# Router rows of twelve tiles: a store, four quarter loads and a VectorE transpose in place of eight TensorE transposes

## The reference, cut to what matters

```python
h2 = rmsnorm(x, g_ffn).reshape(b * s, d)          # (2048, 1024)
logits = h2 @ w_router                            # (2048, 64), float32
scores = sigmoid(logits); idx = top_k(scores + router_bias, 8)
# rows of h2 are then gathered by expert; shared expert and routed experts read h2
```

## Time and profile before

| | us |
|---|---|
| median of three runs | 2726.22 (2724.84 to 2729.26) |
| the profiled execution, its own time | 2727.88 |
| span of the profiled execution | 2726.2 |

### The profile page before, as it was taken

The page is one execution under the profiler, slowest core; times in us unless marked ns, Lnnn a source line. Parts: engine busy times, 40 slices in busy tenths (PEclk is TensorE's granted clock), DMA queues, the critical chain, the costliest instruction groups (busy, mean ns, idle before and its releaser), DMA issues.

```text
span 2726.2 us, 51142 instructions
## 1 busy us (share of the span) xinstructions
PE 2622.2 (96%) x11902; PEld 2165.7 (79%) x11903; DVE 1795.3 (66%) x2519; ACT 1222.6 (45%) x1738; POOL 1311.7 (48%) x1111
## 2 busy tenths in 40 slices
PE   7999999999999999938999999999999999999997
PEld 6888888878887888736888888888888888888885
DVE  4544555646555655557777887777877777777576
ACT  3223323222323223215666665665666655556422
POOL 3000003200122013167877887787887877878711
PEclk9999999999999999959999999999999999999998
DMA  8223433442343333427898998888988988888665
GB/s 314 94 94 107 146 101 100 124 146 92 100 131 116 124 109 108 147 77 256 266 276 240 295 269 242 239 247 255 278 265 240 274 235 239 235 235 243 185 244 195
DMA packets 169902, 523.52 MB, mean 192 GB/s; under 512 B 37706, under 2 KB 43516, under 8 KB 169856
## 3 DMA queue, kind: packets, MB, share of 16 engines
q1 hardware_dynamic: 95776, 344.42, 35.3%
q0 software_dynamic: 65872, 164.37, 25.3%
q10 hardware_dynamic: 8208, 14.16, 1.5%
HBM read 434.94 MB, written 119.18 MB: 203 GB/s over the span
## 4 chain that ended last, share of the span: by engine, by line
PE 48%; DVE 2%; issue 2%; POOL 1%; DMA 1%; ACTq 1%; ACT 1%; DVEq 0%; POOLq 0%; another core or an unknown queue 0%; SPq 0%
PE ps_gu L1479 10%; PE ps_gu L1481 10%; PE ps_gu L1480 10%; PE ps_y L1481 5%; PE ps_y L1480 5%; PE ps_y L1479 5%; PE ps_h L1526 1%; POOL xs L1414 1%; ACTq L1638 1%; DVE xt L1671 0%; DVE xl L1682 0%; DMA xs<-h_dram,gidx 0%; ACT xh L1556 0%; DVE y L1743 0%; DVE expert_raw L1743 0%
## 5 line engine op out<-in xcount | busy, mean ns | idle before, releaser
L1414 POOL DMA_INDIRECT xs<-h_dram,gidx x656 | 819.8, 1250 | 202.1 <-issue 199.0
L1479 PE MATMUL ps_gu<-expert_hi,xl 128*128 (+1 forms) x1392 | 544.1, 391 | 22.6 <-DVE xl L1682 18.1
L1481 PE MATMUL ps_gu<-expert_hi,xh 128*128 (+1 forms) x1392 | 544.1, 391 | 0.0
L1480 PE MATMUL ps_gu<-expert_lo,xh 128*128 (+1 forms) x1392 | 543.5, 390 | 0.0
L1666 DVE TENSOR_TENSOR expert_lo<-expert_raw,expert_hi 128x1024 f32 (+1 forms) x390 | 459.5, 1220 | 120.3 <-ACT expert_hi L1556 82.7
L923 DVE TENSOR_TENSOR ul<-raw,uh 128x1024 fp32r<-128x1024 f32 x186 | 227.9, 1225 | 403.5 <-ACT uh L747 381.0
L1556 ACT ACTIVATE expert_hi<-expert_raw 128x1024 f32 (+1 forms) x390 | 390.6, 1051 | 62.7 <-PEq L1530 38.5
L94 POOL TENSOR_SCALAR rstd<-mean 128x1 f32<-128x1 f32 x45 | 11.1, 246 | 826.6 <-ACT junk L766 812.6
L510 PE MATMUL ps_t<-hh,ul 128*128 128x512 f32 x1024 | 402.7, 393 | 3.1 <-DVE wgl L1152 3.1
L511 PE MATMUL ps_t<-hl,uh 128*128 128x512 f32 x1024 | 400.3, 391 | 0.0
L512 PE MATMUL ps_t<-hh,uh 128*128 128x512 f32 x1024 | 400.0, 391 | 0.0
(11 more groups left out here) (266 smaller groups left out, 3940.0 us busy)
## 6 DMA issues: line engine op xcount, KB each, us to landing
expert_raw<-experts SPq DMA_DIRECT2D x396, 512.0 KB
raw<-units SPq DMA_DIRECT2D x192, 512.0 KB
xs<-h_dram,gidx POOLq DMA_INDIRECT x656
h_dram<-h ACTq DMA_DIRECT2D x17, 512.0 KB
acc_odd<-h POOLq DMA_DIRECT2D x17, 512.0 KB, 14.6
acc<-x SPq DMA_DIRECT2D x4, 2048.0 KB, 8.2
expert_raw<-acc_odd SPq DMA_DIRECT2D x16, 512.0 KB, 4.7
expert_raw<-x POOLq DMA_DIRECT2D x14, 512.0 KB, 3.7
```

The lines of the kernel that those rows point to most:

```text
L1414: nc.gpsimd.indirect_dma_start(xs[s][:, g * DQ:(g + 1) * DQ], None, h2_quarters, bass.IndirectOffsetOnAxis(ap=gidx[s][:, g:g + 1], axis=0) ...
L1479: nc.tensor.matmul(out_, sl, vh, start=first, stop=False)
L1480: nc.tensor.matmul(out_, sh, vl, start=False, stop=False)
L1481: return nc.tensor.matmul(out_, sh, vh, start=False, stop=last)
```

## The change

The twelve tiles in the loops no longer use TensorE to be turned. When `h2` is written, GpSimd stores it to its place in DRAM, waits for that store, and loads it back into `h2` by four DMAs, one for each quarter of the columns, so that row quarters and column quarters lie as a 32x32 block transpose wants them. VectorE then writes `h2t` by one transpose (`y_turn`), after the third `split_lo` of half d = 0. The router weights for these tiles lie in the matching order; SyncE loads the plain order again before the last four tiles, which are turned as before.

```diff
 (SyncE, after the last chunk's unit loads)
+            sp.wait_ge(logits_done, NT - TT + 1)
+            carry(sp, marks)
+            sp.dma_start(wr[:, :, :], w_router[1]).then_inc(wr_in, 16)
 (GpSimd)
+            def y_rows(n):
+                pool.wait_ge(y_normed, n + 1)
+                carry(pool, marks)
+                pool.dma_start(h2_tiles[ds1(n)].rearrange("a p d -> p (a d)"), h2[:, :]).then_inc(h2_stored, 16)
+                pool.wait_ge(h2_stored, n * 16 + 16)
+                carry(pool, marks)
+                for q in range(Q):
+                    pool.dma_start(h2[q * P // Q:(q + 1) * P // Q, :].rearrange("p (g d) -> p g d", g=Q),
+                                   h2_tiles[ds1(n), :, q * D // Q:(q + 1) * D // Q].rearrange(
+                                       "a (g p) d -> p (a g) d", g=Q)).then_inc(h2_quartered, 16)
             def routed(before):
                 n = before * TT
                 y_norm(n)
+                y_rows(n)
                 with pool.Fori(0, TT - 1) as i:
                     y_norm(i + (n + 1))
+                    y_rows(i + (n + 1))
                     scatter(i + n)
 (TensorE, front)
-                        if before is not None and d == 0:
-                            turn_y(i + before * TT)
 (TensorE, tail)
+                pe.wait_ge(wr_in, 16)
                 turn_y(n)
 (ScalarE, front; y_copy stays for the last four tiles)
-                        if before is not None and d == 0:
-                            y_copy(i + before * TT)
 (VectorE)
             def y_scale(i, n, col=YCOL):
                 dve.wait_ge(y_rstd, n + 1)
-                dve.wait_ge(h2_out, n * 16 + 16)
+                dve.wait_ge(h2_out, 16 * max(n - (NCH - 1) * TT, 0) + 16 if isinstance(n, int) else 16)
+            def y_turn(n):
+                dve.wait_ge(h2_quartered, n * 64 + 64)
+                dve.wait_ge(logits_done, n + 1)
+                V.transpose(h2t[:, :, :].rearrange("p k (g t) -> p g k t", g=Q),
+                            h2[:, :].rearrange("p (g k t) -> p g k t", g=Q, k=KD)).then_inc(y_copied, 1)
                         split_lo(ub + (k + 4), k + 2)
+                        if before is not None and d == 0:
+                            y_turn(i + before * TT)
 (host layout)
-        "w_router": np.ascontiguousarray(slices(a["w_router"])),
+        "w_router": np.stack([quarters(a["w_router"]), slices(a["w_router"])]),
```

More of the change, by code:

```diff
@@ L283, in route @@
         y_copied = sem("y_copied")
+        h2_stored = sem("h2_stored")
+        wr_in = sem("wr_in")
+        h2_quartered = sem("h2_quartered")
         logits_done = sem("logits_done")
@@ L351, in _ @@
                              (iota_e, iotas[1, :, 0:NE]),
-                             (gffn, g_ffn), (wr, w_router), (rbias, router_bias)):
+                             (gffn, g_ffn), (wr, w_router[0]), (rbias, router_bias)):
                 sp.dma_start(dst[tuple(slice(None) for _ in src.shape)], src).then_inc(const_in, 16)
@@ L781, in y_copy @@
             def y_copy(n):
-                act.wait_ge(y_turned, n + 1)
+                act.wait_ge(y_turned, n - (NCH - 1) * TT + 1)
                 act.wait_ge(logits_done, n + 1)
@@ L787, in y_copy @@
                 last.then_inc(y_copied, 1)
-                act.dma_start(h2_tiles[n] if isinstance(n, int) else
-                              h2_tiles[ds1(n)].rearrange("a p d -> p (a d)"),
-                              h2[:, :]).then_inc(h2_out, 16)
+                act.dma_start(h2_tiles[n], h2[:, :]).then_inc(h2_out, 16)
             def score(n):
@@ L912, in _ @@
             score(n + 3)
-            act.wait_ge(h2_out, 16 * NT + 16)
+            act.wait_ge(h2_out, 16 * TT + 16)
         @block.vector
```

## The result

The changed kernel takes 2838.87 us (median, 2837.32 to 2843.26) against 2726.54 before: ratio 1.0416, 95% interval 1.0403 to 1.0428. It is 112 us slower; the forecast was +67, with a range up to 2822. The direction and the place were right, the size was not. Its profiled execution has a span of 2841.4 us, 115.2 more than that of the kernel before.

The account below looks back on a forecast made before the run. TensorE, busy 96% of the span, was taken to bound the kernel. Nine tiles at 5.95 us (53.6) and three at 4.35 (13.0) add 66.6 to 2727.9: 2794.5 profiled, forecast 2793 us, range 2761 to 2822.

Parts of the forecast that it names:

- transposes removed: On TensorE in the loops: eight transposes a tile gone, 0.88 us saved in each of 12 tiles, 10.6 us.
- place behind the split, first tiles: At the router: the transpose queued on VectorE behind the third `split_lo` makes it 3.73 us late in three tiles.
- split and round trip, second and third tiles: At the router: 3.73 us late behind the split, plus 1.2 us for the trip through DRAM.
- the same, fourth tiles: At the router: again 3.73 us behind the split plus 1.2 us for the DRAM trip, no longer than in other tiles.
- clock: TensorE behind each stall: granted clock falls to 0.50, losing 1.5 us in three tiles and 1.9 in nine.
- Traffic and scatters: 12 MB of added DMA and the previous tile's scatters, now later on GpSimd, were to cost nothing.
- The trip in an undisturbed tile: Store of `h2` to DRAM and four quarter loads back, until VectorE wakes: 10.2 us, bounds 7.7 and about 13.5.
- VectorE's wake: Last step of the DRAM trip, VectorE starting after the quarter loads land: an estimate of 0.3 us.
- the 0.6 us that the prediction allowed for this: GpSimd's store issue under `split_lo`: if VectorE locks out descriptor writing, up to 0.6 us more in nine trips.
- nine wait 10.2 - 9.0 = 1.2 us more: At the router: the DRAM trip, 10.2 us against 9.0 available, adds 1.2 us (0 to 4.5) in nine tiles.
- Rival (D): The DRAM trip is long, 13 us, as quarters land late or issues stretch: +96, 2822 us; chance 0.17.
- 0.09 more for the change of shape: On TensorE after the transposes: the second matmul follows after 0.32 us, usually 0.23; counted in the 0.88 us removed.

Follow-up runs that it names:

- experiment 4: The changed kernel with VectorE's transpose one place earlier, ahead of the third split of half d = 0: 2824.46 us, ratio 1.0365 against the kernel before.
- (5): The kernel before, with the store moved to GpSimd and four quarter loads into a buffer that nothing reads, TensorE's transposes kept: 2728.66 us, ratio 1.0010.
- experiment 1: The changed kernel with SyncE's 2 MB residual load issued behind the first two unit loads of `back`: 2819.22 us, ratio 1.0332 against the kernel before.
- Experiment 3: The changed kernel with TensorE waiting at the same place, but running the next gate unit before the router: 2830.58 us, ratio 1.0376 against the kernel before.

## Why the prediction was wrong

Its steps, with what the trace and the runs put in their place:

| step | forecast, us | measured, us |
|---|---|---|
| transposes removed | -10.6 | -9.6 (six branch units wait for a split, 0.16 each) |
| place behind the split, first tiles | 3 x 3.73 | 3 x 3.80 |
| split and round trip, second and third tiles | 6 x 4.93 | 32.7 (31.7 idle and 6 x 0.16) |
| the same, fourth tiles | 3 x 4.93 | 39.6 (39.1 idle and 3 x 0.16) |
| clock | 21.6 | 39.6 |
| sum | +66.6 | +113.7, of 115.2 between the two spans |

**What held.** The router stands still in all twelve tiles. The wait has two causes and they divide as stated: experiment 4 takes it out of first tiles alone, of two of the three. Traffic and scatters cost nothing that can be told (5). The trip in an undisturbed tile was sized within 0.6 us, and not by errors that cancel: 0.81 us to the store, 4.67 from there to the first quarter load and 5.36 to the transpose, against 0.6, 4.4 and 5.2. The 0.3 us for VectorE's wake among these had no row. The store took 0.62 to 0.68 us to issue, also beside the split, against 0.63 in the earlier trace rows: the 0.6 us that the prediction allowed for this did not come.

**The first step that failed: the round trip of the fourth tiles.** The prediction set "nine wait 10.2 - 9.0 = 1.2 us more". Six do, about (1.3 to 1.7); three wait 8.9 to 9.6. I had bounded the trip by landings read elsewhere and had looked at the DMA share of the first iteration only the earlier trace rows. What SyncE issues meanwhile, a unit load and behind it the 2 MB residual load, I had not followed, although the residual load waits for the same count as the changed kernel's own round trip. The trace of the kernel before shows it in the fourth iteration, 6.0 us after `h2` is written at 504.48:

```profile
510.47 0.01 SPq L371 DMA_DIRECT2D x<-x  x1
```

By the steps of the prediction the quarter loads would have been issued from 504.48 + 0.6 + 3.8 + 0.6 = 509.5 to 511.1, on both sides of it. Rival (D) had the right kind of cause, a long trip, but spread evenly and not at a named place: 24.8 us were missing here, and experiment 1 gives them back (23 us).

**The second: the size of the clock's fall.** Mechanism and sign were right; "1.5 us for each of the three and 1.9 for each of the nine" came from two stalls in `back`. Here the low clock holds for about 6.5 us in the first tile, and 3.3 us are lost in the mean of the twelve, 18 us more than forecast in sum. In `back` the eight transposes of 128 columns and then full units followed; here 16 matmuls of 64 columns did. Experiment 3 puts a full unit first, and the loss falls to 1.8 in the first tile, as in `back`, 2.6 in the second and 29.6 in all, so this is 10 of the 18 us. Where the other 8 come from, and why single tiles lose from 1.7 to 4.2 with the same order of work, stays open.

**A small one: the removed transposes.** The 0.88 us took "0.09 more for the change of shape" as gone with them. In six of the twelve tiles the branch unit starts 0.16 us late all the same, because it now waits for VectorE's split: 9.6 us saved and not 10.6.

**The rest.** 1.5 us of the difference of the spans are in none of these terms; they are within what two executions differ by (2835.6 to 2841.4 us for this kernel).

## What to carry to other kernels

Moving work off the busiest engine gains only if the result is ready when that engine's queue comes to it: find the instruction on the new engine that the moved work stands behind, and what releases that one. Here the release was the very unit that had just ended, so 0.88 us saved cost 3.8 to 13 us and the clock. For a new round trip through DRAM, list every transfer that any queue issues while it is under way, tile by tile; one loop iteration of four can be another case. The cure was to move the reader one unit back and the 2 MB load two units back, which costs nothing by itself and lets the saving through.

## What the runs showed of the hardware

- After an idle time of TensorE of 3.6 us or more, with a router of 64-column matmuls behind it, the granted clock fell in all twelve tiles. In the first it was 0.50 for about 6.5 us, 3.3 us lost; over the twelve 1.7 to 4.2 us were lost, and the three tiles with 3.64 us of idle had 3.3, 1.7 and 4.2. The first tile's stall filled with matmuls that nothing reads: 7.77 against 7.68 us, nothing lost.
- With a full unit (24 matmuls of 512 columns) behind stalls of about the same length, 1.5 to 3.0 us were lost, 29.6 in place of 39.6 over twelve tiles.
- The clock also fell for a part behind 1.5 to 2.1 us of idle followed by the router (9.34 to 10.97 us in place of 7.68), in four of six tiles; behind 0.82 us of idle it did not, and behind 2.60 us with full matmuls following it had not either.
- Four quarter loads of 128 KB, issued 0.24 to 0.46 us behind a 2 MB load on another queue, landed after 8.6, 9.1 and 8.8 us (medians in the three loops; 11.1 at most), against a median of 3.5 over all 48. The 2 MB load took 17.2 us in the median, and 10.6 when it was issued later (experiment 1).
- A 512 KB store issued by GpSimd landed after 4.2 us (3.0 to 4.5). GpSimd issued its four quarter loads in 2.37 us, and started the store 0.8 us after the VectorE result that it waited for.
